# GLA values with tokens on partitions, and their grid rows regrouped into columns through DRAM

## The chip, the core and the metric

The kernel runs on one core of one Trainium2 chip. The metric is the device time of one execution in microseconds (us), lower is better.

## What is computed

The reference is one layer of a diffusion backbone over 512 latent tokens (a grid of 8 rows by 64 columns) with a prefix of 256 context tokens, width 1024, all in float32. A SwiGLU half step comes first, then token mixing (an S5 branch and a gated linear attention branch, GLA, on the same normalised input), then a second SwiGLU half step. The change touches the values `v` of the GLA branch:

```python
u_l, q_l, k_l, v_l, r_l, glr_l, ga_l, gb_l = jnp.split(h_lat @ w_in, points, axis=-1)
u_c, q_c, k_c, v_c, r_c, glr_c, ga_c, gb_c = jnp.split(h_ctx @ w_in, points, axis=-1)
...
q_l, k_l, v_l, r_l, glr_l = [to_col_major(t, rows) for t in (q_l, k_l, v_l, r_l, glr_l)]
...
kv = jnp.einsum('bhnjd,bhnje->bhnde', k * jnp.exp(g_last - gc), v)
...
o_intra = jnp.einsum('bhnij,bhnje->bhnie', scores, v)
```

GLA walks the grid column by column, so the latent tokens of `v` (512 tokens by 512 channels) must stand in the order of columns (token `8*w + r` for column `w` and row `r`), while `h` holds them row by row (`64*r + w`). The products above contract over tokens, so `v` is wanted with tokens on the partitions. Context tokens keep their order.

## The kernel before

Every float32 product is split in three: the operands are cut into a high and a low part in fp32r, and high times low, low times high and high times high are added up in PSUM. `h` is kept as `h_hi` and `h_lo`, 128 partitions of channels by 8 blocks `k` by 768 tokens (512 latent, then 256 context). Weights arrive in units of 128 x 1024 floats: SyncE's queue (SP) loads `w_raw` (four slots), GpSimd (POOL) cuts it into `w_hi` and `w_lo` (L1177 and L1180), TensorE (PE) uses them. A unit's load waits until the unit four before has been cut (`w_split`), its cutting waits until PE is done with the unit four before. PSUM's eight banks are four slots of two banks; a job `j` uses slot `j % 4` (`lat(j)` and `ctx_(j)` are its banks), `job_done` counts finished jobs, and `slot_read` says that a slot was read.

The order of the work on each engine is written out by hand. Around the change PE's program is: the gate logits of two passes (L1811), four jobs `v`, the first half `u0` of the S5 input (`input_part(0)`), the jobs `vt`, and then the list `GLA_ORDER`, which begins with `ket 0` (transposes of the decayed keys), `sc 0` (scores, L1846), `u 1`, `kv 0` (keys times values, L1862), `u 2` and so on.

The four jobs `v` (`tall_job`, all matmuls recorded at L1276) hold the weights still and move the tokens: for each of 4 x 8 blocks and 3 parts one matmul over 512 latent and one over 256 context tokens, 96 pairs in all. The result has channels on the partitions. ScalarE (ACT) copies it to `v_t` and puts the grid in column order by the way (`evac_tokens`, L2394 and L2396). Then 24 PE transposes (L1287, the jobs `vt`) turn it, and ACT copies it to `v_sb` (`take_v`, L2441), from where `kv` and later the readout (L1876) take it.

Other transfers through DRAM that the prediction reads: `g_scr` keeps gates (one transfer writes 128 partitions of 512 floats), and `k_scr` keeps S5 kernels, which SP reads with a hand-made pattern whose leading dimension is `CH = 8`:

```python
lags = bass.AP(k_scr.tensor, (b * P + STRIP * g) * 15 * GC, [[GC, CH], [15 * GC, GC], [1, P]])
sp.dma_start(tile[:, 0, g, :], lags).then_inc(here, 16)
```

Of the kernel before, what the change touches and what calls it, by code (L numbers as in the profile page):

```python
# [29 lines left out]
F32 = mybir.dt.float32  # L30
# [6 lines left out]
P = 128  # L37
# [194 lines left out]
def y_load(h, b):  # L232
# [5 lines left out]
              ("ffn1", FFN1_JOBS), ("norm1", 0), ("q0", 1), ("q1", 1), ("glr", 1), ("k", 2), ("z0", 1), ("z1", 1),  # L238
              ("v", 4), ("u0", 1), ("vt", 6), ("gla", GLA_JOBS), ("chunks", 23), ("gb", 6), ("ga", 8), ("merge", len(MERGE_ORDER)),
              ("ma", KD), ("wo", KD), ("ada7", 1), ("wo_b", 4), ("ffn2", FFN2_JOBS),  # L240
# [117 lines left out]
def last_user(n):  # L358

    for name, count, jobs in (("k", 2, JOB["k"]), ("q0", 1, JOB["q0"]), ("glr", 1, JOB["glr"]), ("q1", 1, JOB["q1"]), ("v", 4, JOB["v"]),  # L360
                              ("ga", 8, JOB["ga"]), ("wo", 4, JOB["wo"])):
        if UNIT[name] <= n < UNIT[name] + count:
            return jobs + n - UNIT[name]
# [30 lines left out]
def build(nc, a, out):  # L394
# [4 lines left out]
    x_scr = nc.dram_tensor("x_scr", [P, KD, NL], F32).ap()  # L399
    u_scr = nc.dram_tensor("u_scr", [CH, GC, G, NCH], F32).ap()  # L400
    g_scr = nc.dram_tensor("g_scr", [P, 2 * KD, NL], F32).ap()

# [107 lines left out]
    g_d = place("g_d", [P, NT], F32, at=stream_at + 9 * KB)  # L510
    v_t = place("v_t", [P, 4, NT], F32, at=ut_at)
    gate_buf = place("gate_buf", [P, 2, NL], F32, at=v_at + 8 * KB)
# [225 lines left out]
    with ExitStack() as es:  # L738
        def sem(name):
            return es.enter_context(nc.semaphore(name))  # L740
# [61 lines left out]
        hc_hi_ok = sem("hc_hi_ok")  # L802
        hc_ok = sem("hc_ok")
        xn_ok = sem("xn_ok")
        h_hi_ok = sem("h_hi_ok")
# [76 lines left out]
        def product_done(eng, q, i):  # L882

            eng.wait_ge(product_ok, NPROD * q + i + 1)

        def block_consumed(eng, b):
# [35 lines left out]
        def _(sp):  # L922
# [100 lines left out]
            def tall(n, count, c0, c=P):  # L1023
                for q in range(count):
                    unit(n + q, w_in[:, :, c0 + q * P:c0 + q * P + c], raw((n + q) % 4, KD, c))

            def load_gate(t):
                g, s = (gate_a, gate_a_in) if t < KD else (gate_b, gate_b_in)
                sp.dma_start(g[:, t % KD, :], g_scr[:, t, :]).then_inc(s[t % KD], 16)
# [24 lines left out]
            tall(UNIT["k"], 2, C_K)  # L1054
            tall(UNIT["v"], 3, C_V)


            sp.wait_ge(xn_ok, 2 * KD)
            sp.dma_start(x_scr, x[:, :, 0:NL]).then_inc(x_spilled, 16)
            tall(UNIT["v"] + 3, 1, C_V + 3 * P)  # L1060
            tall(UNIT["u"], 4, C_U)
            for q, t in enumerate(R_ORDER):
                tall(UNIT["r"] + q, 1, C_R + t * P)
            tall(UNIT["gb"], 2, C_GB)
# [101 lines left out]
        def _(pool):  # L1166
# [16 lines left out]
            def split(n, cols):  # L1183
                pool.wait_ge(w_here[n % 4], 16 * (n // 4 + 1))
                is_done(pool, last_user(n - 4))
                parts(n % 4, cols, n + 1)
# [75 lines left out]
        def _(pe):  # L1262
# [459 lines left out]

            def input_part(p):

                q, j = p // 2, GJ["u", p]
                n, c = UNIT["u"] + q, slice(NL, NT) if p % 2 else slice(0, NL)
                if p % 2 == 0:
                    pe.wait_ge(w_split, n + 5)
                wait_read(pe, j)
                wh, wl = wv(n % 4, KD, P)  # L1730
                split_mm([(wh[:, k, :], wl[:, k, :], [(h_hi[:, k, c], h_lo[:, k, c], lat(j)[:, 0:c.stop - c.start])])
                          for k in range(KD)]).then_inc(job_done, 1)

# [84 lines left out]
            gate_logits(1)  # L1818
            for q in range(4):
                tall_job("v", q, JOB["v"] + q, NT)  # L1820
            input_part(0)
            for q in range(4):
                was_read(pe, JOB["v"] + q)
            for t in range(6):
                j = JOB["vt"] + t
                wait_read(pe, j)
                for q in range(4):
                    last = transpose(lat(j)[:, P * q:P * q + P], v_t[:, q, P * t:P * t + P])
                last.then_inc(job_done, 1)
            def turn_keys(p):  # L1830
# [19 lines left out]
            def key_values(p):  # L1850
                ti, d = p // 2, p % 2
                was_read(pe, GJ["ket", p])
                order = (4, 5, 0, 1, 2, 3) if d == 0 else (5, 4, 3, 2, 1, 0)
# [321 lines left out]
        def _(act):  # L2175
# [261 lines left out]

            def take_v(t):
                j = JOB["vt"] + t
                is_done(act, j)  # L2440
                act.activation(v_sb[:, t, :], lat(j), ACT.Copy).then_inc(slot_read[j % 4], 1)  # L2441

# [39 lines left out]
            softplus(1)  # L2482
            evac_tokens(JOB["v"], v_t[:, 0, :], NT, P)
            decays(0)
            for q in range(1, 4):
                evac_tokens(JOB["v"] + q, v_t[:, q, :], NT, P)
            decays(1)
            take_u(0)
            for t in range(6):
                take_v(t)  # L2490
            take_keys(0)
# [1377 lines left out]
```

## Time and profile before

| | before |
|---|---|
| median of 3 runs | 1352.38 us (1352.18 to 1355.9) |
| the profiled execution | 1354.73 us, of which the profile's span is 1353.0 us |
| mean granted TensorE clock | 0.997 |
| busy share: PE, DVE, ACT, POOL | 99%, 64%, 29%, 48% |
| DMA | 178.18 MB, mean 132 GB/s |

Times in the rows are us from the start of the span. A row of the timeline merges neighbours of one kind: start, duration, engine, line, operation, output and inputs, count, and in brackets the idle time before it. The duration of a matmul reaches over the start of the next one, since they are pipelined; what a stream of them costs is read from start to start.

### The profile page before, as it was taken

How to read it: one execution, taken by the hardware profiler on the slowest of the kernel's cores; microseconds unless marked ns; L12 is line 12 of the kernel's file. 1: busy time of each engine (PE TensorE's matmuls, PEld its weight loads, DVE VectorE, ACT ScalarE, POOL GpSimd, SP SyncE). 2: the span in 40 equal slices, each digit the busy share in tenths (PEclk: the TensorE clock that was granted, in tenths of full speed). 3: DMA queues.
4: the chain of work that ended last, by engine and by line, in shares of the span. 5: the costliest groups of instructions: out<-in, count | busy, mean ns of one | idle time of the engine just before them, and what ended most of it. 6: DMA issues, size and time to landing. Idle time of an engine off the chain costs nothing.

```text
span 1353.0 us, 21483 instructions
## 1 busy us (share of the span) xinstructions
PE 1335.8 (99%) x8556; PEld 1232.3 (91%) x8556; DVE 864.3 (64%) x1383; ACT 395.8 (29%) x750; POOL 652.2 (48%) x408
## 2 busy tenths in 40 slices
PE   7999999999999999999999999999999999999998
PEld 5899999999999999998888888888998999999997
DVE  5697368468556555537656649926778755555666
ACT  4310010210210110124635321222142555544455
POOL 3164444543543543532732356636567455655554
PEclk9999999999999999999999999999999999999999
DMA  9653354353454344223322479484736233344322
GB/s 319 199 148 91 119 147 125 113 159 115 126 140 134 106 128 152 63 55 109 81 61 51 129 211 260 152 268 145 229 87 199 63 94 94 109 116 114 99 75 82
DMA packets 242798, 178.18 MB, mean 132 GB/s; under 512 B 33288, under 2 KB 219916, under 8 KB 242700
## 3 DMA queue, kind: packets, MB, share of 16 engines
q1 hardware_dynamic: 222640, 145.78, 37.7%
q10 hardware_dynamic: 20060, 31.04, 7.0%
q8 instruction: 68, 1.11, 0.4%
q14 instruction: 30, 0.25, 0.1%
HBM read 156.93 MB, written 19.86 MB: 131 GB/s over the span
## 4 chain that ended last, share of the span: by engine, by line
PE 92%; DVE 4%; ACT 1%; issue 1%; ACTq 0%; DMA 0%; POOL 0%; DVEq 0%; POOLq 0%
PE ps L1276 46%; PE ps L2041 13%; PE ps L1636 13%; PE ps L2100 7%; PE ps L1287 1%; PE ps L1914 1%; DVE ada_acc L2924 1%; DVE ps L3028 1%; PE ps L2127 1%; PE ps L1951 1%; PE ps L1739 1%; PE ps L1531 1%; PE ps L1482 1%; PE ps L1776 1%; ACT squares L2197 0%
## 5 line engine op out<-in xcount | busy, mean ns | idle before, releaser
L1177 POOL TENSOR_SCALAR w_hi<-w_raw 128x1024 fp32r<-128x1024 f32 x128 | 154.7, 1209 | 526.8 <-PE ps L1276 279.4
L1180 POOL TENSOR_TENSOR w_lo<-w_raw,w_hi 128x1024 fp32r<-128x1024 f32 x128 | 325.0, 2539 | 10.7
L1276 PE MATMUL ps<-h_hi,w_lo 128*128 128x384 f32 (+2 forms) x984 | 287.3, 351 | 0.0
L1276 PE MATMUL ps<-h_hi,w_hi 128*128 128x384 f32 (+2 forms) x984 | 283.0, 346 | 0.0
L1276 PE MATMUL ps<-h_lo,w_hi 128*128 128x384 f32 (+2 forms) x984 | 283.0, 346 | 0.0
L1276 PEld LDWEIGHTS ps<-h_hi,w_lo 128*128 128x128 f32 x984 | 175.8, 188 | 14.9 <-issue 4.3
L1276 PEld LDWEIGHTS ps<-h_hi,w_hi 128*128 128x128 f32 x984 | 177.6, 188 | 10.8
L1276 PEld LDWEIGHTS ps<-h_lo,w_hi 128*128 128x128 f32 x984 | 177.8, 188 | 10.4
L1254 POOL TENSOR_TENSOR w_lo<-w_raw,w_hi 128x512 fp32r<-128x512 f32 x90 | 115.8, 1301 | 104.4 <-ACT w_hi L2673 102.9
L2924 DVE SCALAR_TENSOR_TENSOR ada_acc<-ada_w,cs,ada_acc 128x1024 f32<-128x1024 f32 x70 | 114.5, 1671 | 6.0 <-DMA ada_w<-in_ada_w_dram 4.0
L2041 PE MATMUL ps<-h_hi,w_hi 128*128 128x256 f32 x360 | 102.0, 283 | 0.0
L2041 PE MATMUL ps<-h_hi,w_lo 128*128 128x256 f32 x360 | 101.9, 283 | 0.0
L2041 PE MATMUL ps<-h_lo,w_hi 128*128 128x256 f32 x360 | 101.8, 283 | 0.0
L1636 PE MATMUL ps<-act_hi,w_lo 128*128 128x384 f32 (+1 forms) x352 | 94.7, 343 | 0.3 <-DVE x L3303 0.3
L1636 PE MATMUL ps<-act_hi,w_hi 128*128 128x384 f32 (+1 forms) x352 | 94.0, 341 | 0.0
L1636 PE MATMUL ps<-act_lo,w_hi 128*128 128x384 f32 (+1 forms) x352 | 94.0, 341 | 0.0
L2315 ACT ACTIVATE silu<-ps 128x768 f32<-128x768 f32 (+1 forms) x26 | 20.3, 780 | 199.3 <-PE ps L1276 193.0
L2334 ACT ACTIVATE act_hi<-ps 128x768 fp32r<-128x768 f32 (+2 forms) x26 | 20.0, 769 | 190.9 <-DVE ps L3259 190.8
L3301 DVE SCALAR_TENSOR_TENSOR x<-ps,mod,x 128x384 f32<-128x384 f32 (+2 forms) x120 | 49.1, 476 | 31.6 <-PE ps L1636 31.5
L2041 PEld LDWEIGHTS ps<-h_hi,w_lo 128*128 128x128 f32 x360 | 68.9, 191 | 0.3
L2041 PEld LDWEIGHTS ps<-h_lo,w_hi 128*128 128x128 f32 x360 | 68.8, 191 | 0.3
L2041 PEld LDWEIGHTS ps<-h_hi,w_hi 128*128 128x128 f32 x360 | 68.8, 191 | 0.0
(452 smaller groups left out, 2648.1 us busy)
## 6 DMA issues: line engine op xcount, KB each, us to landing
w_raw<-in_ffn_w_gate_dram SPq DMA_DIRECT2D x44, 512.0 KB, 5.0
w_raw<-in_ffn_w_up_dram SPq DMA_DIRECT2D x44, 512.0 KB, 4.1
w_raw<-in_ffn_w_down_dram SPq DMA_DIRECT2D x44, 512.0 KB, 3.9
ada_w<-in_ada_w_dram ACTq DMA_DIRECT2D x32, 512.0 KB, 3.9
w_raw<-in_w_in_dram SPq DMA_DIRECT2D x32, 512.0 KB, 4.1
ada_w<-in_ada_w_dram SPq DMA_DIRECT2D x24, 512.0 KB, 4.0
ada_q<-in_ada_w_dram SPq DMA_DIRECT2D x8, 1024.0 KB, 10.7
c_scr<-cp ACTq DMA_DIRECT2D x16, 288.0 KB, 3.7
```

The lines of the kernel that those rows point to most:

```text
L1177: pool.tensor_scalar(w_hi[:, s, 0:cols], w_raw[:, s, 0:cols], 1.0, 1.0, ALU.mult, ALU.mult)\
L1180: pool.tensor_tensor(w_lo[:, s, 0:cols], w_raw[:, s, 0:cols], w_hi[:, s, 0:cols].bitcast(F32), ALU.subtract).then_inc(w_split, 1)
L1254: pool.tensor_tensor(lo, src, hi.bitcast(F32), ALU.subtract).then_inc(block_lo, 1)
L1276: last = pe.matmul(mv[2], st, mv[part], start=(first and q == 0), stop=(n == len(terms) - 1 and q == 2))
L1287: return pe.transpose(o, i, ident[0:i.shape[0], 0:i.shape[0]])
L1636: last = pe.matmul(bank, st[:, k, c], mv[:, k, cols], start=(k == 0 and r == 0), stop=(k == tiles - 1 and r == 2))
L2041: last = pe.matmul(bank_of(q, bank), st[:, k, :], mv[:, k, :], start=(opens and k == 0 and r == 0), stop=(closes and k == HK - 1 and r == ...
L2100: last = pe.matmul(ps[:, banks[e], :], st[:, k, c], mv[:, f + k, 0:NL], start=(k == 0 and r == 0), stop=(k == 1 and r == 2))
L2315: act.activation(dst, src, ACT.Silu).then_inc(slot_read[jg % 4], 1)
L2334: act.activation(dst, src, ACT.Copy).then_inc(act_hi_ok, 1)
L2924: STT(acc, tile, cs[:, k, v:v + 1], acc, ALU.mult, ALU.add).then_inc(acc_ok, 1)
L3301: ins = STT(x[:, k, c], src, mod[:, g, v:v + 1], x[:, k, c], ALU.mult, ALU.add)
```

## The change

The values are made with `h` held still and the weights moving. The four weight units of `v` are cut the other way: two blocks `k` of 512 columns each, in place of eight blocks of 128 columns. For each unit PE runs over six tiles of 128 tokens, with 2 x 3 matmuls of 512 columns each, 144 in all, into six PSUM banks (three slots) that stay open over the four units. The result has tokens on the partitions, so the 24 transposes go. What the copy by ACT did before, the order by columns, is now made by DMA: ACT copies the four latent tiles to `v_row` as they are, SP writes them to `v_scr` in DRAM in four transfers, with rows of 512 floats put at their place in column order, and when all four have landed SP reads `v_scr` back into `v_sb` in four transfers. The two context tiles are copied to `v_sb` directly. `kv 0` waits for the eight transfers.

```diff
-              ("v", 4), ("u0", 1), ("vt", 6), ("gla", GLA_JOBS), ...
+              ("v", 3), ("v_pad", 2), ("u0", 1), ("u0_pad", 1), ("gla", GLA_JOBS), ...
+    v_scr = nc.dram_tensor("v_scr", [NL, VAL], F32).ap()
-    v_t = place("v_t", [P, 4, NT], F32, at=ut_at)
+    v_row = place("v_row", [P, 4, VAL], F32, at=ut_at)
+        def values_read(q):
+            return q + 1 if q < 3 else 6
+        def values_made(m):
+            return 4 + m
+            def value_unit(q):
+                n = UNIT["v"] + q
+                unit(n, w_in[:, 2 * q:2 * q + 2, C_V:C_V + VAL], raw(n % 4, 2, VAL))
+            def turn_values():
+                by_row = v_scr.rearrange("(w r) c -> r w c", r=ROWS)
+                for m in range(2):
+                    was_read(sp, JOB["v"] + m)
+                    for t in (2 * m, 2 * m + 1):
+                        sp.dma_start(by_row[2 * t:2 * t + 2], v_row[:, t, :]).then_inc(v_here, 16)
+                sp.wait_ge(v_here, 16 * 4)
+                for t in range(4):
+                    sp.dma_start(v_sb[:, t, :], v_scr[P * t:P * t + P, :]).then_inc(v_here, 16)
...
             for q, t in enumerate(R_ORDER):
+                if q == 3:
+                    turn_values()
                 tall(UNIT["r"] + q, 1, C_R + t * P)
...
-                is_done(pool, last_user(n - 4))
+                q = n - 4 - UNIT["v"]
+                if 0 <= q < 4:
+                    pool.wait_ge(v_ok, values_read(q))
+                else:
+                    is_done(pool, last_user(n - 4))
...
+            def values():
+                for q in range(4):
+                    n = UNIT["v"] + q
+                    wh, wl = [w[:, n % 4, :].rearrange("p (k c) -> p k c", k=2) for w in (w_hi, w_lo)]
+                    pe.wait_ge(w_split, n + 5)
+                    for t in range(6):
+                        j = JOB["v"] + t // 2
+                        if q == 0 and t % 2 == 0:
+                            wait_read(pe, j)
+                        o = (lat, ctx_)[t % 2](j)
+                        for k in range(2):
+                            for r, (h, w) in enumerate(((h_hi, wl), (h_lo, wh), (h_hi, wh))):
+                                last = pe.matmul(o, h[:, 2 * q + k, P * t:P * t + P], w[:, k, :], start=(q == 0 and k == 0 and r == 0),
+                                                 stop=(q == 3 and k == 1 and r == 2))
+                        if t == 5 or (q == 3 and t % 2 == 1):
+                            last.then_inc(v_ok, 1)
...
-            for q in range(4):
-                tall_job("v", q, JOB["v"] + q, NT)
-            input_part(0)
-            for q in range(4):
-                was_read(pe, JOB["v"] + q)
-            for t in range(6):
-                j = JOB["vt"] + t
-                wait_read(pe, j)
-                for q in range(4):
-                    last = transpose(lat(j)[:, P * q:P * q + P], v_t[:, q, P * t:P * t + P])
-                last.then_inc(job_done, 1)
+            values()
+            input_part(0, JOB["gla"] - JOB["v"])
...
             def key_values(p):
+                if p == 0:
+                    pe.wait_ge(v_here, 16 * 8)
...
+            def take_v(m):
+                j = JOB["v"] + m
+                act.wait_ge(v_ok, values_made(m))
+                dst = v_row[:, 2 * m:2 * m + 2, :] if m < 2 else v_sb[:, 4:6, :]
+                first = act.activation(dst[:, 0, :], lat(j), ACT.Copy)
+                if m == 2:
+                    first.then_inc(slot_read[(j + 1) % 4], 1)
+                act.activation(dst[:, 1, :], ctx_(j), ACT.Copy).then_inc(slot_read[j % 4], 1 if m == 1 else 2)
...
-            evac_tokens(JOB["v"], v_t[:, 0, :], NT, P)
             decays(0)
-            for q in range(1, 4):
-                evac_tokens(JOB["v"] + q, v_t[:, q, :], NT, P)
+            take_v(0)
+            take_v(1)
             decays(1)
+            take_v(2)
             take_u(0)
-            for t in range(6):
-                take_v(t)
```

The instructions themselves show it at three places. On PE, where the values are made, the stream began before with these rows (`h` moves, 512 and 256 wide; brackets hold the semaphores waited for):

```order
L1276 MATMUL ps<-h_hi,w_lo 128x512 [waits slot_read3,w_split]
L1276 MATMUL ps<-h_hi,w_lo 128x256
L1276 MATMUL ps<-h_lo,w_hi 128x512
L1276 MATMUL ps<-h_lo,w_hi 128x256
L1276 MATMUL ps<-h_hi,w_hi 128x512
L1276 MATMUL ps<-h_hi,w_hi 128x256
```

and now begins with these, where the weights move, 512 wide:

```order
L1768 MATMUL ps<-w_lo,h_hi 128x512 [waits slot_read3,w_split]
L1768 MATMUL ps<-w_hi,h_lo 128x512
L1768 MATMUL ps<-w_hi,h_hi 128x512
L1768 MATMUL ps<-w_lo,h_hi 128x512
L1768 MATMUL ps<-w_hi,h_lo 128x512
L1768 MATMUL ps<-w_hi,h_hi 128x512
```

Every pair of 512 and 256 has become one and a half matmuls of 512; the columns moved are as many as before.

On PE between `u0` and `kv 0`, the transposes of `v_t` stood ahead of those of the keys (`ke`):

```order
L1287 MATMUL ps<-ident,v_t 128x128 [waits slot_read0]
L1287 MATMUL ps<-ident,v_t 128x128 x3
L1287 MATMUL ps<-ident,v_t 128x128 [waits slot_read1]
L1287 MATMUL ps<-ident,v_t 128x128 x3
L1287 MATMUL ps<-ident,ke 128x128 [waits slot_read2,e_d]
L1287 MATMUL ps<-ident,ke 128x128 x5
L1846 MATMUL ps<-e1q,kz 128x128 [waits slot_read3,e_d]
L1846 MATMUL ps<-e1q,kz 128x128 x7
```

They are gone, and the first product of keys and values, behind the last matmuls of `u 1`, now waits for the transfers too (`v_here`):

```order
L1308 MATMUL ps<-h_hi,w_lo 128x256
L1308 MATMUL ps<-h_lo,w_hi 128x256
L1308 MATMUL ps<-h_hi,w_hi 128x256
L1905 MATMUL ps<-v_sb,ket 64x128 [waits slot_read1,slot_read2,v_here]
L1905 MATMUL ps<-v_sb,ket 64x128 x11
L1905 MATMUL ps<-v_sb,ket 64x128 [waits slot_read2]
L1905 MATMUL ps<-v_sb,ket 64x128 x11
```

Everything that PE has behind that row stands behind the wait.

On SP's queue, from the loads of the values' weights on, it was (the shape is that of the side written):

```order
L926 DMA w_raw<-in_w_in_dram 128x8x128 [waits w_split] x5
L1059 DMA x_scr<-x 1024x1x512 [waits xn_ok]
L926 DMA w_raw<-in_w_in_dram 128x8x128 [waits w_split] x11
L1070 DMA u_scr<-u_t 16x8x96 [waits slot_read0,slot_read3]
L1070 DMA u_scr<-u_t 16x8x96 x7
```

and is now:

```order
L1085 DMA x_scr<-x 1024x1x512 [waits xn_ok]
L937 DMA w_raw<-in_w_in_dram 128x2x512 [waits w_split]
L937 DMA w_raw<-in_w_in_dram 128x8x128 [waits w_split] x7
L1047 DMA v_scr<-v_row 2x64x512 [waits slot_read3]
L1047 DMA v_scr<-v_row 2x64x512
L1047 DMA v_scr<-v_row 2x64x512 [waits slot_read0]
L1047 DMA v_scr<-v_row 2x64x512
L1050 DMA v_sb<-v_scr 128x512 [waits v_here]
L1050 DMA v_sb<-v_scr 128x512 x3
L937 DMA w_raw<-in_w_in_dram 128x8x128 [waits w_split] x3
L1098 DMA u_scr<-u_t 16x8x96 [waits slot_read0]
```

Eight transfers have moved in ahead of the last three weight loads of this stage, and the four that write have a leading dimension of 2 on the DRAM side.

## Rows read from the trace of the kernel before

**Rows 1.** The page: busy tenths of PE and granted clock in 40 slices.
```profile
PE   7999999999999999999999999999999999999998
PEclk9999999999999999999999999999999999999999
```

**Rows 2.** The chain that ended last, 650 to 700 us: start, us, what.
```profile
653.38 39.62 PE ps L1276 x216
692.99 3.28 PE ps L1287 x30
696.27 1.09 PE ps L1846 x16
```

**Rows 3.** Timeline of PE: first values, `u0`, transposes, keys, `u 1`, `kv 0`.
```profile
653.31 0.62 PE L1276 MATMUL ps<-h_hi,w_lo 128*128 128x512 f32 x2
...
687.32 0.40 PE L1276 MATMUL ps<-h_hi,w_lo 128*128 128x512 f32 x1
...
692.83 2.78 PE L1287 MATMUL ps<-ident,v_t 128*128 128x128 f32 x24
695.45 0.82 PE L1287 MATMUL ps<-ident,ke 128*128 128x128 f32 x6
...
700.34 1.54 PE L1862 MATMUL ps<-v_sb,ket 64*64 64x128 f32 x48
```

**Rows 4.** The chain, 798 to 876 us: a stream of matmuls, all 512 wide.
```profile
798.44 76.24 PE ps L1276 x336
```

**Rows 5.** Weight loads into PE at L1276: ns min/median/max.
```profile
L1276 PEld LDWEIGHTS ps<-h_hi,w_lo x984: 186/188/192, 65.7 to 1035.5; 128*128 128x128 f32 x197
```

**Rows 6.** Timeline of ACT: copies of `v_sb`, and the second pass's decays.
```profile
688.84 0.61 ACT L2432 ACTIVATE g_a<-g_b 128x512 f32<-128x512 f32 x1
...
690.86 0.61 ACT L2436 ACTIVATE g_c<-g_c 128x512 f32<-128x512 f32 x1
...
693.52 3.04 ACT L2441 ACTIVATE v_sb<-ps 128x512 f32<-128x512 f32 x6
```

**Rows 7.** Timeline of POOL: cutting the unit `u2`, before `r2` may load.
```profile
679.17 1.05 POOL L1177 TENSOR_SCALAR w_hi<-w_raw 128x1024 fp32r<-128x1024 f32 x1 [4.38 <-PE ps L1276]
680.31 2.70 POOL L1180 TENSOR_TENSOR w_lo<-w_raw,w_hi 128x1024 fp32r<-128x1024 f32 x1
```

**Rows 8.** Loads of L926 (512 KB each), 640 to 700 us: min/median/max to landing.
```profile
DMA to landing us min/median/max: 3.9/4.0/5.5
```

**Rows 9.** DMA from 862 to 868 us: one gate write of 256 KB, alone.
```profile
GB/s 0 0 0 0 0 0 0 0 0 0 0 0 0 0 0 0 0 0 0 0 55 14 314 382 396 410 219 14 0 0 0 0 0 0 0 0 0 0 0 0
DMA packets 145, 0.27 MB, mean 45 GB/s; under 512 B 16, under 2 KB 16, under 8 KB 144
q10 hardware_dynamic: 144, 0.26, 11.7%
```

**Rows 10.** DMA from 883.3 to 885.0 us: the last four `k_scr` reads (64 KB each).
```profile
DMA  7669554546555656645493444446655435499978
DMA packets 546, 0.28 MB, mean 164 GB/s; under 512 B 32, under 2 KB 545, under 8 KB 545
```

**Rows 11.** Timeline of SP: those four issues, and eight gate reads.
```profile
881.12 2.47 SPq L1043 DMA_DIRECT2D stream<-k_scr  x4
...
902.71 3.66 SPq L1029 DMA_DIRECT2D gate_a<-g_scr  x8
```

**Rows 12.** All DMA issues by line: KB each, median us to landing.
```profile
gate_a<-g_scr SPq DMA_DIRECT2D x8, 256.0 KB, 4.4
```

**Rows 13.** Windows near the start: us, busy (count) PE PEld DVE ACT POOL, PEclk, DMA.
```profile
13.00:16.60 3.60, 0.83 (x5) 0.57 (x5) 2.19 (x6) 3.55 (x9) 1.57 (x2) 1.00 1.10 358
16.60:20.05 3.45, 3.45 (x24) 2.79 (x28) 0.91 (x3) 3.00 (x7) 1.82 (x1) 0.51 1.12 339
20.05:23.50 3.45, 3.42 (x42) 2.22 (x34) 3.45 (x5) 0.77 (x2) 0.71 (x1) 1.00 1.19 298
```

**Rows 14.** Waits of the weight loads, whole span: what PE waited for.
```profile
PEld ps L1951 <- DVE hb L3686: 0.4, 1, 0.4
```

More of the change, by code:

```diff
@@ L238 @@
               ("ffn1", FFN1_JOBS), ("norm1", 0), ("q0", 1), ("q1", 1), ("glr", 1), ("k", 2), ("z0", 1), ("z1", 1),
-              ("v", 4), ("u0", 1), ("vt", 6), ("gla", GLA_JOBS), ("chunks", 23), ("gb", 6), ("ga", 8), ("merge", len(MERGE_ORDER)),
+              ("v", 3), ("v_pad", 2), ("u0", 1), ("u0_pad", 1), ("gla", GLA_JOBS), ("chunks", 23), ("gb", 6), ("ga", 8), ("merge", len(MERGE_ORDER)),
               ("ma", KD), ("wo", KD), ("ada7", 1), ("wo_b", 4), ("ffn2", FFN2_JOBS),
@@ L358, in last_user @@
 def last_user(n):
-    for name, count, jobs in (("k", 2, JOB["k"]), ("q0", 1, JOB["q0"]), ("glr", 1, JOB["glr"]), ("q1", 1, JOB["q1"]), ("v", 4, JOB["v"]),
+    for name, count, jobs in (("k", 2, JOB["k"]), ("q0", 1, JOB["q0"]), ("glr", 1, JOB["glr"]), ("q1", 1, JOB["q1"]),
                               ("ga", 8, JOB["ga"]), ("wo", 4, JOB["wo"])):
@@ L803, in build @@
         hc_ok = sem("hc_ok")
+        v_ok = sem("v_ok")
+        v_here = sem("v_here")
         xn_ok = sem("xn_ok")
@@ L1054, in _ @@
             tall(UNIT["k"], 2, C_K)
-            tall(UNIT["v"], 3, C_V)
+            for q in range(3):
+                value_unit(q)
             sp.wait_ge(xn_ok, 2 * KD)
             sp.dma_start(x_scr, x[:, :, 0:NL]).then_inc(x_spilled, 16)
-            tall(UNIT["v"] + 3, 1, C_V + 3 * P)
+            value_unit(3)
             tall(UNIT["u"], 4, C_U)
             for q, t in enumerate(R_ORDER):
+                if q == 3:
+                    turn_values()
                 tall(UNIT["r"] + q, 1, C_R + t * P)
@@ L1721, in tall_job, with input_part @@
                 split_mm(tall_terms(name, q, j, toks, c)).then_inc(job_done, 1)
-            def input_part(p):
+            def values():
[14 more added lines that the diff above has]
+                            last.then_inc(v_ok, 1)
+            def input_part(p, jobs=1):
                 q, j = p // 2, GJ["u", p]
@@ L1731, in input_part @@
                 split_mm([(wh[:, k, :], wl[:, k, :], [(h_hi[:, k, c], h_lo[:, k, c], lat(j)[:, 0:c.stop - c.start])])
-                          for k in range(KD)]).then_inc(job_done, 1)
+                          for k in range(KD)]).then_inc(job_done, jobs)
             def latents(name, q, j, c, k0, k1):
@@ L2436, in decays @@
                 act.activation(g_c[:, 0:NL], g_c[:, 0:NL], ACT.Exp, scale=1.0 / 16).then_inc(e_a, 1)
[L2438 to L2441, printed above, removed]
+            def take_v(m):
[6 more added lines that the diff above has]
+                act.activation(dst[:, 1, :], ctx_(j), ACT.Copy).then_inc(slot_read[j % 4], 1 if m == 1 else 2)
             def take_keys(p):
```

## The prediction

> **What bounds the kernel now.** I read the page's slices first: PE is at nine tenths or more in 38 of 40, with the clock granted in full [rows 1]. Then the chain of work that ended last, at the place of the change: it runs along PE without a break, 39.62 us of matmuls at L1276, then 3.28 us of transposes, then the scores [rows 2]. So the kernel's time is PE's own time here: whatever PE is spared is saved, and whatever makes PE wait is paid in full, since no other engine stands behind it with work of its own to lose. Third, PE's timeline [rows 3]. It is read from start to start: the values take from 653.31 to 687.32, which is 34.0 us for 96 pairs; `u0` takes 5.51 us to 692.83; the 24 transposes of `v_t` take 2.62 us to 695.45; keys, scores and `u 1` follow, and `kv 0`, the first user of `v_sb`, starts at 700.34.
>
> **What PE is spared.** The 24 transposes go: 2.6 us. The values become 144 matmuls of 512 columns. A stream of such runs 336 times in 76.24 us, 0.227 us each [rows 4], and `u0` ran 24 in 5.51 us, 0.230 each [rows 3]: 32.7 to 33.1 us, I take 32.8. That saves 1.2 us of the 34.0, although the columns are the same. `h` as the operand held still must be loaded for each matmul, but the weights were too, in 188 ns [rows 5], which fits under 227 ns. Together 3.8 us. All that follows would move forward by as much: `kv 0` would be due at 696.5.
>
> The Trainium skill (TensorE: Matmul & The Clock Gate, section Back-to-back issue gap) gives the isolated gap between matmuls as columns over 2.4 GHz plus 2.5 ns. By it the old stream would be 31.2 us and the new 31.1, so that the regrouping alone gave 0.1 us; the rows show 34.0 and 32.7 at least, so I go by the rows.
>
> **Work of other engines.** ACT loses the copies to `v_t` and gets six of about 0.5 us [rows 6], fewer than before; POOL cuts the same units. The values' banks are complete at 680.6, 683.4 and 686.1 (the fourth unit runs from 677.9 to 686.1, two tiles each 2.7 us). ACT needs about 1.1 us for each of the two latent pairs, so slots are released at 681.9 and 684.6. The second pass's decays (2.6 us from 688.84 to the end of the row at 690.86 [rows 6]) come behind them and then the context pair, at about 688.4; the slot that `ket 0` wants at 691.6 is free by then. None of this reaches PE. DVE's instructions are the same.
>
> **The eight transfers.** SP must first issue the load of unit `r2`, which waits until `u2` is cut. That cut took 3.8 us from its start at 679.17 [rows 7]; it now starts at 677.9, so the load is issued at 681.8 and its data is through at about 685.2 (4.0 us to landing [rows 8], less a little for the completion). The writes of tiles 0 and 1 are issued at 682 behind it in the same queue, those of 2 and 3 at 684.7.
>
> How long do the writes take? A gate write of the same size and the same rows of 2 KB, alone in its window, moves 128 packets of data and 16 under 512 B, and uses 11.7% of 16 engines over 6.0 us: 11.2 us of one engine's time, at up to 410 GB/s [rows 9]. The 16 small packets I take for one completion by each engine that took part. Spread over 16 engines that is 0.7 us. But the `k_scr` reads, whose pattern in DRAM leads with a dimension of 8, look otherwise: in 1.7 us the last four leave 32 small packets beside 513 others (4 x 128 rows of 512 B), eight each and not sixteen, and the DMA row stands at about half [rows 10]. They were issued within 2.5 us [rows 11] and drained together, and still only half the engines worked: each takes eight engines, and the four take the same eight. So a transfer here uses as many engines as the leading dimension allows, and a second one gets no others. The four writes of `v_row` lead with 2 (`2x64x512`, two grid rows). I therefore expect them on two engines, all four on the same two: 4 x 11.2 / 2 = 22.3 us.
>
> The Trainium skill (DMA: Bandwidth & Descriptors, section Why a DMA increments its semaphore by 16 and not by 1) says that a transfer issued from SP runs on the largest number of engines up to 16 that divides the leading dimensions of both sides, and on the lowest-numbered ones. The 32 small packets agree with it. By that rule 2 and 128 give two engines, and the writes take the same 22.3 us.
>
> Then the sum: the writes have the two engines from about 685.2 to 707.5, landed 707.8. SP issues the four reads (128 partitions, all engines); eight such reads were issued in 3.66 us [rows 11], landing 4.4 us after issue at the median under each other's load [rows 12]. Between 2.6 us (1 MB at 410 GB/s and nothing else) and 5.8 us (three issues of 0.46 and 4.4) I take 4.2: `v_sb` is there at 712.0, while `kv 0` was due at 696.5. PE stands still for 15.5 us; behind it in its queue is everything else, so the stall is paid in full. Nothing makes it up: SP's later loads `r3` and `gb` are held to 708 as well, but PE wants them only some 50 us further on.
>
> **The clock.** PE does not stand still for so long anywhere in this trace. After sparse work (0.83 us busy of 3.60) and a wait, the granted clock was 0.51 for 3.45 us, the lower of the two levels, 1.2 GHz, and then 1.00 again [rows 13]. I expect one such stretch when PE starts again: 3.45 us at half pace, 1.7 us lost. Bounds: nothing, and two stretches, 3.4 us.
>
> **Sum.** -3.8 + 15.5 + 1.7 = +13.4 us. The profile's own span of 1353.0 would be 1366.4; its execution took 1354.73, 2.35 us above the median of the runs. Against the median of 1352.38 I forecast 1366 us.
>
> **The rivals.**
> *The writes spread.* If they ran on all 16 engines, each takes 0.7 us of transfer, they land before 688 and `v_sb` is there by 693, ahead of 696.5. The same if eight engines serve them (5.6 us, reads landed at about 695.5), or if each write had a pair of its own. Then only the 3.8 us remain: 1348.6. For it speaks that the count of 2 lies outside what the trace shows (the least dimension seen is 8) and that I know the pattern from the program's text; against it the 32 small packets and the half-used engines [rows 10]. It decides at 6.8 us for the four writes: from 685.2 they then land at 692.3, the reads at 696.5, and nothing is exposed; at about 10.6 us the stall would just eat the 3.8.
> *The writes use two engines each, but at another pace.* The 2 KB rows might go at 410 GB/s over 16 engines, the peak of [rows 9]: 20.5 us for the four. Or at the pace of [rows 10] (256 KB on 8 engines in 1.7 us, 19.3 GB/s an engine): 27.2 us. I take [rows 9], the same shape and direction. The ends: 20.5 us of writes, 2.6 of reads and no clock loss give a stall of 12.1 and +8.3; 27.2, 5.8 and 3.4 give a stall of 22.0 and +21.6.
> *The operand exchange is slower than the rows say.* If `h` held still cost more than 227 ns, say 5% of 32.8, then 1.6 us more; with the writes hidden that is 1350.2, no measurable change. Loads of 188 ns speak against it [rows 5].
> *DVE becomes the bound.* PE waits only 0.4 us for the S5 scan (`hb`) [rows 14]. But the scan starts from PE's results too, and moves with them: no price.
>
> **How the numbers follow.** Two engines, all four writes on them: 0.88. Spread or otherwise hidden: 0.09, of which half is measured as over 0.3% faster, since 3.8 us is 0.28%. Something between (partly exposed, near zero): 0.03. A measurement tells 0.3%, 4.1 us, from no change. Faster 0.05, same 0.06, slower 0.89. The likeliest case's own range is 1360 to 1371: its lower end is the cheap bounds, its upper leaves out most of the way to +22, since the packets of [rows 9] have the shape in question. It holds about 9 in 10 of that case, which makes 8 in 10 of all.
>
> **What would show it.** In the profile after: 144 matmuls of 512 at 0.227 us and no `v_t`; `u0` starting near 686.1; four writes landing 13 to 23 us after their issue, with the DMA share near an eighth; a gap of some 15 us on PE before `kv 0` at about 696.5, put down to DMA; a granted clock of 0.5 behind it; all later stages as before. I am wrong if the writes land in 2 to 4 us, each with 16 small packets, or if PE's gap is under 8 us.

## The result, and the profile after

The changed kernel takes 1369.17 us (median of 6 runs, 1367.95 to 1372.63); the kernel before took 1353.99 us in its 6 runs beside it (1352.18 to 1355.9). The ratio is 1.0114, with a 95% interval of 1.0100 to 1.0127: slower by some 15.4 us. The profiled execution, 1372.51 us, is one of the longer of the six; its span is 1370.8 us, against 1353.0 before.

The page of the changed kernel, PE and granted clock in 40 slices, and the chain that ended last by engine:

```profile
PE   6999999999999999999949999999999999999998
PEclk8999999999999999999979999999999999999999
...
PE 91%; DVE 4%; DMA 2%; ACT 1%; issue 1%; ACTq 1%; SPq 1%; POOL 0%; DVEq 0%; POOLq 0%
```

One slice is 34 us. Where all slices but the first and the last were 9 [rows 1], one now is 4, and the clock beside it 7. All the rest is as before, so the question has one place. The chain of the changed kernel there, 650 to 725 us (start, us, what):

```profile
654.62 24.76 PE ps L1768 x108
...
679.53 1.89 POOL w_hi L1205
...
681.49 2.73 POOL w_lo L1208
...
684.23 0.37 SPq L937
...
684.64 0.64 SPq L1047
...
685.33 1.10 SPq L1047
...
686.48 3.64 SPq L1047
...
690.16 18.46 DMA v_scr<-v_row
...
708.63 0.35 SPq L1050
...
709.98 5.26 DMA v_sb<-v_scr
...
715.28 2.84 PE ps L1905 x48
718.12 6.58 PE ps L1308 x24
```

The chain leaves PE at 679.4 and comes back to it at 715.28. It goes over POOL's cut of `u2`, SP's load of `r2` behind it (L937), the four writes (L1047), 18.46 us of waiting for the last of them, and the four reads (L1050). Then `kv 0` (L1905) starts, and takes 2.84 us where it took some 1.5 [rows 3]. What PE waited for (us in total, times, longest):

```profile
PEld ps L1905 <- DMA v_sb<-v_scr: 17.7, 1, 17.7
PE ps L1905 <- DMA v_sb<-v_scr: 17.5, 1, 17.5
```

The windows of the same stretch (busy and count of PE, PEld, DVE, ACT, POOL; granted clock, DMA share, GB/s):

```profile
688.00:693.00 5.00, 5.00 (x24) 4.09 (x24) 0.00 (x0) 1.45 (x3) 3.14 (x2) 1.00 0.13 51
...
698.00:703.00 5.00, 0.00 (x0) 0.00 (x0) 1.88 (x2) 0.19 (x1) 3.99 (x2) 1.00 0.13 51
703.00:708.00 5.00, 0.00 (x0) 0.00 (x0) 0.00 (x0) 0.00 (x0) 0.00 (x0) 0.50 0.13 51
...
715.00:720.00 5.00, 4.72 (x53) 4.00 (x54) 2.65 (x8) 0.00 (x0) 0.00 (x0) 0.50 0.38 104
720.00:725.00 5.00, 5.00 (x26) 4.13 (x25) 2.34 (x5) 0.26 (x1) 0.00 (x0) 1.00 0.00 0
```

Read the last two columns first. From 688 to 708 the DMA engines are 0.13 busy, two of sixteen (0.125), and move 51 GB/s, some 26 GB/s for each of the two. Then the column before them: PE stopped at 697.75, the granted clock is 0.50 (1.2 GHz) from 703 on, and still is for nearly five microseconds after PE has started again. How many engines a write took can be counted too. DMA of 683 to 709 us:

```profile
DMA packets 1560, 1.57 MB, mean 60 GB/s; under 512 B 24, under 2 KB 1048, under 8 KB 1560
```

In that window `r2`'s load and the four writes end. 24 small packets are 16 for the load and 8 for the writes, two each.

### The profile page after: what moved, and what is told of

Same layout as the page of the kernel before. It is cut to its first block, busy times and chain, and to the rows that moved or that the text cites. A ratio compares the mean times of both kernels' runs of the same rounds, so it can differ in the third digit from the quotient of the medians.

```text
span 1370.8 us, 21334 instructions
## 1 busy us (share of the span) xinstructions
PE 1334.5 (97%) x8484; PEld 1231.4 (90%) x8484; DVE 865.0 (63%) x1383; ACT 390.3 (28%) x742; POOL 653.6 (48%) x408
## 4 chain that ended last, share of the span: by engine, by line
PE 91%; DVE 4%; DMA 2%; ACT 1%; issue 1%; ACTq 1%; SPq 1%; POOL 0%; DVEq 0%; POOLq 0%
PE ps L1308 43%; PE ps L2084 13%; PE ps L1668 13%; PE ps L2143 7%; PE ps L1768 2%; PE ps L1563 1%; DMA v_scr<-v_row 1%; PE ps L1319 1%; PE ps L1957 1%; DVE ada_acc L2970 1%; DVE ps L3074 1%; PE ps L2170 1%; PE ps L1994 1%; PE ps L1789 1%; PE ps L1514 1%
## 5 line engine op out<-in xcount | busy, mean ns | idle before, releaser
L1308 PE MATMUL ps<-h_hi,w_lo 128*128 128x384 f32 (+2 forms) x920 | 271.0, 352 | 0.0
L1308 PE MATMUL ps<-h_hi,w_hi 128*128 128x384 f32 (+2 forms) x920 | 266.8, 347 | 0.0
L1308 PE MATMUL ps<-h_lo,w_hi 128*128 128x384 f32 (+2 forms) x920 | 266.7, 347 | 0.0
L1308 PEld LDWEIGHTS ps<-h_hi,w_lo 128*128 128x128 f32 x920 | 166.3, 188 | 13.3 <-issue 3.9
L1308 PEld LDWEIGHTS ps<-h_hi,w_hi 128*128 128x128 f32 x920 | 168.0, 188 | 9.3
L1308 PEld LDWEIGHTS ps<-h_lo,w_hi 128*128 128x128 f32 x920 | 168.1, 188 | 8.9
L2358 ACT ACTIVATE silu<-ps 128x768 f32<-128x768 f32 (+1 forms) x26 | 20.3, 780 | 199.3 <-PE ps L1308 193.0
L2084 PEld LDWEIGHTS ps<-h_hi,w_lo 128*128 128x128 f32 x360 | 68.9, 191 | 0.3
L2084 PEld LDWEIGHTS ps<-h_lo,w_hi 128*128 128x128 f32 x360 | 68.8, 191 | 0.3
L2084 PEld LDWEIGHTS ps<-h_hi,w_hi 128*128 128x128 f32 x360 | 68.8, 191 | 0.0
```

Of the source, the lines that this page charges most:

```text
L1308: last = pe.matmul(mv[2], st, mv[part], start=(first and q == 0), stop=(n == len(terms) - 1 and q == 2))
L2084: last = pe.matmul(bank_of(q, bank), st[:, k, :], mv[:, k, :], start=(opens and k == 0 and r == 0), stop=(closes and k == HK - 1 and r == ...
L2358: act.activation(dst, src, ACT.Silu).then_inc(slot_read[jg % 4], 1)
```

## The experiments

One theory and its rivals ran through them. The theory: the leading dimension of a transfer sets how many DMA engines it runs on, and the data of the most loaded engine go through at 26 GB/s. The rivals: the round trip through DRAM is late by itself; rows that lie 16 KB apart are slow to write; the many issues cost SP the time; another queue would use other engines. Ratios are to the kernel before, with their 95% intervals.

**Writes of single grid rows.** Same bytes to the same places, but each transfer leads with 64.

```diff
-                    for t in (2 * m, 2 * m + 1):
-                        sp.dma_start(by_row[2 * t:2 * t + 2], v_row[:, t, :]).then_inc(v_here, 16)
-                sp.wait_ge(v_here, 16 * 4)
+                    for r in range(4 * m, 4 * m + 4):
+                        sp.dma_start(by_row[r], v_row[64 * (r % 2):64 * (r % 2) + 64, r // 2, :]).then_inc(v_here, 16)
+                sp.wait_ge(v_here, 16 * 8)
...
-                    pe.wait_ge(v_here, 16 * 8)
+                    pe.wait_ge(v_here, 16 * 12)
```

> Each of the four writes of two grid rows (2x64x512) becomes two writes of one grid row (64x512, 128 KB); the reads stay. Theory (a transfer runs on as many engines as its leading dimension allows, 2 before, 16 now): the eight writes take about 0.35 us of 16 engines each, landed some 4 us after the last is issued, so v_sb is complete near PE's due time and the stall of 17.5 us before kv 0 is 0 to 3 us; no stretch at clock 0.5. Time about 3.8 us under before's, 1350, ratio to before 0.997, at most 1.000. Rival 1 (the round trip through DRAM itself is late, or rows of 2 KB that lie 16 KB apart in DRAM are slow): 128 rows of 2 KB are written to the same places, so the writes still take some 20 us and the time stays at ratio 1.011. Rival 2 (more issues cost SP what the engines save): eight issues of 0.6 to 5 us hold SP until past 700, stall 5 to 15 us, ratio 1.002 to 1.010.

Measured: 1351.53 us, ratio 0.9976 (0.9964 to 0.9988). Its chain, 650 to 760 us:

```profile
653.81 32.91 PE ps L1768 x144
686.72 5.44 PE ps L1308 x24
...
693.91 3.05 PE ps L1308 x24
696.96 1.47 PE ps L1905 x48
698.43 5.71 PE ps L1308 x24
```

PE never leaves the chain: `kv 0` follows `u 1` at once, at full clock. SP's timeline, and the DMA packets of 683.8 to 690.8 us:

```profile
683.83 5.09 SPq L1047 DMA_DIRECT2D v_scr<-v_row  x8
690.76 1.77 SPq L1050 DMA_DIRECT2D v_sb<-v_scr  x4
```

```profile
DMA packets 1680, 1.57 MB, mean 225 GB/s; under 512 B 144, under 2 KB 1168, under 8 KB 1680
```

144 small packets are 16 for the load of `r2` and 128 for eight writes, sixteen each. The writes are through 6.9 us after the first was issued, not 24.0. Both rivals fall: the same round trip costs nothing, and eight issues took 5.09 us, half of what four took before.

**No transfers at all.** ScalarE copies straight to `v_sb`. This kernel leaves out the order by columns, so it doesn't compute what the reference does; only its time is read.

```diff
-                dst = v_row[:, 2 * m:2 * m + 2, :] if m < 2 else v_sb[:, 4:6, :]
+                dst = v_sb[:, 2 * m:2 * m + 2, :]
...
-                    turn_values()
+                    pass
...
-                    pe.wait_ge(v_here, 16 * 8)
+                    pass
```

> Leaves out the regrouping of grid rows into columns: ScalarE copies all four value tiles straight to v_sb, the eight transfers and the wait on them are gone, everything else is the change's. It prices the operand exchange and the missing transposes alone. Theory (my terms): 2.6 us of transposes and 1.2 us of values are saved and nothing is lost, 3.8 us under before, ratio 0.9972 (0.9965 to 0.998). Rival (the exchange of the operands costs something that the trace hides, such as h held still loading slower): ratio 0.999 or above. If the whole loss of the change came from elsewhere than the transfers, the ratio would still be 1.011.

Measured: 1349.89 us, ratio 0.9966 (0.9954 to 0.9979). The chain has the same pieces as the run above, 43.15 us from the first value to `kv 0`:

```profile
651.67 32.91 PE ps L1768 x144
...
696.29 5.71 PE ps L1308 x24
```

So the exchange of the operands and the missing transposes are worth 47.03 - 43.15 = 3.9 us [rows 3], and the interval reaches from 2.8 to 6.2. The whole loss of the change lies in the transfers. The intervals of this run and of the one before it overlap, and both take 43.15 us over this stretch: done by grid rows, the transfers cost nothing here that can be measured.

**Near rows, still two by two.** The scratch tensor gets 65 rows for each grid row, so that a grid row's data lie together. This kernel too leaves out the order by columns: `v_sb` then holds rows of the grid.

```diff
-        v_scr = nc.dram_tensor("v_scr", [NL, VAL], F32).ap()
+        v_scr = nc.dram_tensor("v_scr", [ROWS, GRID_W + 1, VAL], F32).ap()
...
-                by_row = v_scr.rearrange("(w r) c -> r w c", r=ROWS)
...
-                        sp.dma_start(by_row[2 * t:2 * t + 2], v_row[:, t, :]).then_inc(v_here, 16)
+                        sp.dma_start(v_scr[2 * t:2 * t + 2, 0:GRID_W, :], v_row[:, t, :]).then_inc(v_here, 16)
...
-                for t in range(4):
-                    sp.dma_start(v_sb[:, t, :], v_scr[P * t:P * t + P, :]).then_inc(v_here, 16)
+                for r in range(8):
+                    sp.dma_start(v_sb[64 * (r % 2):64 * (r % 2) + 64, r // 2, :], v_scr[r, 0:GRID_W, :]).then_inc(v_here, 16)
...
-                    pe.wait_ge(v_here, 16 * 8)
+                    pe.wait_ge(v_here, 16 * 12)
```

> The scratch tensor is laid out as [8 grid rows, 65, 512], so that a grid row's 64 rows of 2 KB lie side by side in DRAM; the four writes still lead with a dimension of 2, and eight reads bring single grid rows back. It leaves out the column order: v_sb holds rows of the grid and not columns. Theory (engine count from the leading dimension): the writes still run on two engines, 20 us, and the time is that of the change, ratio to before 1.009 to 1.013. Rival (the scattered places, 16 KB apart, are what makes the writes slow): with rows side by side the writes take 1 to 3 us and the ratio is 0.997 to 1.000.

Measured: 1371.52 us, ratio 1.0127 (1.0108 to 1.0145). Its chain, and a window:

```profile
690.83 18.49 DMA v_scr<-v_row
```

```profile
700.00:705.00 5.00, 0.00 (x0) 0.00 (x0) 0.36 (x1) 0.00 (x0) 2.56 (x1) 0.57 0.13 51
```

18.49 us, 0.13 and 51 GB/s, as with rows 16 KB apart. Where the rows lie in DRAM made no difference.

**62 and 2, 61 and 3, 57 and 7.** Each grid row is written by two transfers, split as the numbers say; only the pair of numbers differs.

```diff
-                    for t in (2 * m, 2 * m + 1):
-                        sp.dma_start(by_row[2 * t:2 * t + 2], v_row[:, t, :]).then_inc(v_here, 16)
-                sp.wait_ge(v_here, 16 * 4)
+                    for r in range(4 * m, 4 * m + 4):
+                        for a0, a1 in ((0, 62), (62, 64)):
+                            p0 = 64 * (r % 2)
+                            sp.dma_start(by_row[r, a0:a1], v_row[p0 + a0:p0 + a1, r // 2, :]).then_inc(v_here, 16)
+                sp.wait_ge(v_here, 16 * 16)
...
-                    pe.wait_ge(v_here, 16 * 8)
+                    pe.wait_ge(v_here, 16 * 20)
```

> Each grid row is written by two transfers, of 62 and of 2 partitions, 16 writes in all. Two forms of the theory are told apart: by the one a transfer takes the largest number of engines up to 16 that divides the leading dimension (62: two engines, as 2), so the data still go through two engines, the writes take about 20 us and the ratio to before is about 1.011, somewhat more if SP's sixteen issues hold it up. By the other it takes 16 or the leading dimension, whichever is less (62: sixteen), the writes land within 3 to 6 us of the last issue and the ratio is 0.997 to 1.003. For both: small packets of completion counted beside the data, 2 for a transfer by the first, 16 by the second.

> As the run with 62 and 2 partitions, but 61 and 3: 61 is a prime number, so by the divisor rule nearly all data go through one engine. Theory: about 1 MB at 26 GB/s is some 40 us instead of 20, v_sb complete near 730, a stall of 33 to 40 us and 2.4 us of half clock: ratio to before 1.024 to 1.029. Rival (the run with 62 was slow for its sixteen issues or for its small writes of 2 partitions and not for the count of engines): the writes take as long as with 62, ratio 1.011 to 1.015.

> Each grid row is written by two transfers, of 57 and of 7 partitions. 57 is 3 times 19, so by the divisor rule the large one runs on three engines and the small one on seven. The most loaded engine carries 8 x (57/3 + 1) rows of 2 KB, 320 KB, at 26 GB/s 12.6 us, where the change's two carry 512 KB each in 20.2. Theory: the stall is 17.5 - 7.6 = 9.9 us and the stretch at half clock remains, as the run with half the dose had it (8.8 us and a clock of 0.5 behind): -3.8 + 9.9 + 2.4 = 8.5, ratio to before 1.0063 (1.005 to 1.008). Rival (any split into an odd number runs on one engine, or sixteen small issues cost the time): the time of the run with 62 or 61, 1.0137 or 1.0266; or, if 57 rows spread over all engines, 0.9976.

Measured: 62 and 2, 1372.12 us, ratio 1.0137 (1.0116 to 1.0159); 61 and 3, 1390.37 us, 1.0266 (1.0248 to 1.0284); 57 and 7, 1364.02 us, 1.0074 (1.0057 to 1.0091). What PE waited for, in this order:

```profile
PE ps L1907 <- DMA v_sb<-v_scr: 17.9, 1, 17.9
```

```profile
PE ps L1907 <- DMA v_sb<-v_scr: 36.0, 1, 36.0
```

```profile
PE ps L1907 <- DMA v_sb<-v_scr: 9.5, 1, 9.5
```

And one window each of the first two, while the writes ran:

```profile
700.00:705.00 5.00, 0.00 (x0) 0.00 (x0) 0.00 (x0) 0.00 (x0) 0.00 (x0) 0.50 0.13 51
```

```profile
705.00:710.00 5.00, 0.00 (x0) 0.00 (x0) 0.00 (x0) 0.00 (x0) 0.00 (x0) 0.50 0.07 26
```

For 57 and 7, the window in which the last writes ran, and the DMA packets of 683 to 703 us:

```profile
695.00:700.00 5.00, 3.75 (x38) 3.42 (x34) 4.11 (x6) 0.90 (x3) 1.09 (x1) 1.00 0.20 77
```

```profile
DMA packets 1632, 1.57 MB, mean 79 GB/s; under 512 B 96, under 2 KB 1120, under 8 KB 1632
```

62 partitions go through two engines (0.13, 51 GB/s), 61 through one (0.07, 26 GB/s), 57 through three (77 GB/s, three times 26), 64 through sixteen. The small packets say the same. For 57 and 7 they are 96: 16 for the load of `r2` and 80 for eight pairs of writes, three and seven each. From the load to the last write the run with 62 and 2 has 48, which is 16 and eight times 2 + 2, and the run with 61 and 3 has 48 too, 16 and eight times 1 + 3. All three runs have sixteen issues, so it isn't their number that sets the wait. Nor is the count of engines the smaller of 16 and the dimension: it is the dimension's largest divisor up to 16. The Trainium skill (DMA: Bandwidth & Descriptors, section Why a DMA increments its semaphore by 16 and not by 1) states for transfers issued from SP that it is the largest number up to 16 that divides the leading dimensions of both sides; the packets and shares here agree for 64, 62, 61, 57, 7, 3 and 2.

**Half the dose.** Tiles 0 and 1 by pairs of grid rows, tiles 2 and 3 by single ones.

```diff
                     for t in (2 * m, 2 * m + 1):
-                        sp.dma_start(by_row[2 * t:2 * t + 2], v_row[:, t, :]).then_inc(v_here, 16)
+                        if m == 0:
+                            sp.dma_start(by_row[2 * t:2 * t + 2], v_row[:, t, :]).then_inc(v_here, 16)
+                        else:
+                            for r in (2 * t, 2 * t + 1):
+                                sp.dma_start(by_row[r], v_row[64 * (r % 2):64 * (r % 2) + 64, t, :]).then_inc(v_here, 16)
-                sp.wait_ge(v_here, 16 * 4)
+                sp.wait_ge(v_here, 16 * 6)
...
-                    pe.wait_ge(v_here, 16 * 8)
+                    pe.wait_ge(v_here, 16 * 10)
```

> Tiles 0 and 1 are written as in the change (two writes of 2x64x512), tiles 2 and 3 by grid rows (four writes of 64x512): half the dose. Theory (data through two engines at some 26 GB/s each, as the change's trace shows): 512 KB take 10 us from 684, so the writes land at about 695 in the change's time, the reads at 699 to 701.5, kv 0 due at 697.5: a stall of 1.5 to 4 us, no clock loss or a small one, and the 3.8 us saved just pay it: ratio to before 0.998 to 1.001. Rival (any two-engine transfer among them delays all, or the loss has a fixed part that doesn't go with the bytes): a stall of 8 us or more, ratio 1.004 to 1.011.

Measured: 1360.71 us, ratio 1.0047 (1.0030 to 1.0064), and

```profile
PE ps L1909 <- DMA v_sb<-v_scr: 8.8, 1, 8.8
```

This lies outside what I had expected of the theory, and within the rival's range. The fault was in my start: I counted the writes from 684, their issue in the changed kernel. But `r2`'s load is ahead of them on every engine until 688, as the windows of the changed kernel show, and the reads took 6.5 us and not 4. Shifted so that the first value is made when it was in the change, the two engines have 11.3 us of data from 688 (the four other writes put 32 KB on each of them too), the last write is seen at 700, the reads at 706.5, and `kv 0` is due at 697.75: 8.8. That it goes with the bytes is shown by the runs together. The wait is worked out here as 17.5 us less what the most loaded engine is spared of the change's 512 KB, at 26 GB/s:

| run | KB on the most loaded engine | at 26 GB/s, us | wait by that, us | measured, us |
|---|---|---|---|---|
| single rows, 64 | 64 | 2.5 | 0 | 0 |
| half | 288 | 11.3 | 8.6 | 8.8 |
| 57 and 7 | 320 | 12.6 | 9.9 | 9.5 |
| the change | 512 | 20.2 | 17.5 | 17.5 |
| 62 and 2 | 512 | 20.2 | 17.5 | 17.9 |
| 61 and 3 | 992 | 39.1 | 36.4 | 36.0 |

The run with two queues, below, carries 512 KB as well and waited 16.9 us. The two runs of about half the dose differ in their issues (6 and 16), and fall on the same line. The change's own row fits by construction; the others are off by 0.4 us at most, so no fixed part larger than that goes with writes on few engines. The 9.9 of the run with 57 was worked out before that run was made.

**Two queues.** ScalarE issues the writes of tiles 2 and 3.

```diff
-                for m in range(2):
-                    was_read(sp, JOB["v"] + m)
-                    for t in (2 * m, 2 * m + 1):
-                        sp.dma_start(by_row[2 * t:2 * t + 2], v_row[:, t, :]).then_inc(v_here, 16)
+                was_read(sp, JOB["v"])
+                for t in (0, 1):
+                    sp.dma_start(by_row[2 * t:2 * t + 2], v_row[:, t, :]).then_inc(v_here, 16)
...
+                if m == 1:
+                    by_row = v_scr.rearrange("(w r) c -> r w c", r=ROWS)
+                    was_read(act, j)
+                    for t in (2, 3):
+                        act.dma_start(by_row[2 * t:2 * t + 2], v_row[:, t, :]).then_inc(v_here, 16)
```

> The writes of tiles 2 and 3 are issued by ScalarE in its own queue, behind its copies; those of tiles 0 and 1 stay with SyncE. Theory (the leading dimension sets the number of engines and it is the same two for every queue): the four writes together still take 20 us on two engines, ratio to before 1.009 to 1.015, above the change's if ScalarE is held up in issuing. Rival (another queue's transfers go to other engines): the two halves run side by side, 10 us, the DMA share is 0.25 and the stall 2 to 5 us: ratio 0.998 to 1.002.

Measured: 1371.80 us, ratio 1.0132 (1.0112 to 1.0153). The wait, and a window in which both queues have writes open:

```profile
PE ps L1904 <- DMA v_sb<-v_scr: 16.9, 1, 16.9
```

```profile
690.00:695.00 5.00, 5.00 (x27) 4.04 (x27) 0.00 (x0) 3.07 (x7) 2.45 (x2) 1.00 0.13 51
```

Still 0.13 and 51 GB/s: the second queue's writes go to the same two engines.

**A clock kept up.** PE gets work in place of the pause: 76 matmuls into a bank that `kv 0` then overwrites.

```diff
                 if p == 0:
+                    wait_read(pe, GJ["kv", p])
+                    for _ in range(76):
+                        pe.matmul(lat(GJ["kv", p]), h_hi[:, 0, 0:P], h_hi[:, 0, 0:NL], start=True, stop=True)
                     pe.wait_ge(v_here, 16 * 8)
```

> The change, plus 76 matmuls of 512 columns on h_hi into kv 0's own bank (overwritten by it), between PE's last matmul and the wait for v_sb: 76 x 0.227 = 17.3 us of work in place of the idle 17.5. It adds work that the reference doesn't ask for. Theory (4.8 us at clock 0.5 behind the pause cost 2.4 us): the clock stays at 1.00, kv 0 takes 1.47 us and not 2.84, u2's 24 matmuls 5.7 and not 6.6, and the time is 2.4 us below the change's, ratio to before 1.0095. Rival (the granted clock falls for another reason, such as the DMA traffic): 0.5 is still granted from 703 on, and as the filling then runs at half pace too, the time is some 10 us or more above the change's, ratio 1.018.

Measured: 1366.36 us, ratio 1.0089 (1.0073 to 1.0105). A window of the former pause, with the writes running, and the chain behind it:

```profile
700.00:705.00 5.00, 5.00 (x24) 4.14 (x23) 0.00 (x0) 0.00 (x0) 0.00 (x0) 1.00 0.13 51
```

```profile
712.19 1.54 PE ps L1908 x48
713.73 5.68 PE ps L1308 x24
```

The granted clock stays at 1.00 although the same writes run, so it is PE's standing still that lowered it. `kv 0` and the 24 matmuls behind it take 7.2 us in place of 9.4 in the changed kernel: the clock cost it 2.2 us. The two ratios' intervals touch, so the trace and not the timing gives this number.

**The reads alone.** SP waits for the four reads before it loads `r3` and `gb`.

```diff
                     sp.dma_start(v_sb[:, t, :], v_scr[P * t:P * t + P, :]).then_inc(v_here, 16)
+                sp.wait_ge(v_here, 16 * 8)
```

> The change, and SyncE waits for its four reads of v_scr before it issues the loads of r3 and gb behind them (those are held 5 us more; PE wants them some 50 us later). In the change the reads took 6.6 us from the first issue, with 1 MB of loads issued directly behind them. Theory (the loads share the engines with the reads and delay them; alone they take 4 to 4.5 us): v_sb is complete 2 us earlier, the stall is 15.5 and not 17.5, ratio to before 1.0100, 2 us below the change's. Rival (the reads' time is their own, three issues and the landing): still 6.6 us, stall 17.5, ratio 1.0114 or, if the later loads become late for PE, more.

Measured: 1370.22 us, ratio 1.0128 (1.0113 to 1.0143), not told from the change's 1.0114. Its chain:

```profile
705.58 0.35 SPq L1050
...
706.92 4.20 DMA v_sb<-v_scr
...
711.16 2.84 PE ps L1906 x48
714.00 6.90 PE ps L1309 x24
```

The reads take 5.5 us from the first issue (705.58 to 711.12) instead of 6.6, and PE waits 16.7 us instead of 17.5. That alone doesn't show that the loads behind them delay the reads. In the other runs that wait for the same four reads, all with `r3` and `gb` issued right behind, these took, from the first issue to the landing that lets `kv 0` start, 5.35 us (61 and 3), 5.6 (57 and 7), 5.7 (two queues), 6.2 (62 and 2, and the filled pause), 6.5 (half the dose) and 6.6 (the change). So 5.5 can be had with the loads behind, and this one execution doesn't decide between the theory and its rival. The forecast of 4 to 4.5 us for reads alone failed. Nor does the microsecond show in the time; part goes to the clock, since the 24 matmuls of `u2` take 6.90 us here and 6.58 in the changed kernel.

## Why the prediction was right, step by step

The forecast was 1366 us, slower, by writes that run on two engines. Times below are set to the execution of before: in the profiled one of the change the first value is made at 654.55 instead of 653.31 [rows 3], 1.2 us later, for reasons ahead of the change.

- **What PE is spared:** 3.8 forecast, 3.9 measured, from the first value to `kv 0`'s due time. 144 matmuls take 32.91 us, 0.229 each; forecast 32.8. The gap rule of the Trainium skill (TensorE: Matmul & The Clock Gate, section Back-to-back issue gap) made 31.1 of it and a saving of 0.1 in the regrouping; neither is what the chain shows.
- **`kv 0` due at 696.5:** 697.75 less 1.2. Right.
- **Two engines, the same two for all four:** right, and shown by the packets (two for each write), the share (0.13), and the runs with 64, 62, 61 and 57 partitions and with the second queue.
- **The writes' time:** 22.3 us forecast from the one gate write [rows 9] (11.2 times four over two is 22.4), 20.3 measured (688.0 to 708.3), near the rival's 20.5 from the peak of the same rows. They started 1.6 us later than forecast. POOL's cut of `u2` took 4.7 us instead of 3.8 [rows 7], 1.89 for `w_hi` where I had read 1.05, and the load of `r2` kept the engines busy for 3.8 us from its issue and not 3.4; the cut also began 0.4 later. So the landing came out within 0.4 us of the forecast (708.6 against 709.0) by two errors that cancel, which is luck: the writes were forecast 2.0 us too long and 1.6 too early.
- **The reads:** the term that was mis-sized. 4.2 us forecast, 6.6 measured, over my upper bound of 5.8. With nothing behind them they took 5.5, and with the loads behind them between 5.35 and 6.6 in different runs, so what the loads add is not shown. The median landing of gate reads [rows 12] counts from the issue of each, and my bound of 5.8, three issues and one such landing, is near what most runs took; the 4.2 was a choice between two bounds and came out too low.
- **The stall:** 15.5 forecast, 17.5 measured: the reads' 2.4 less the 0.4.
- **The clock:** 1.7 forecast, 2.2 measured. One stretch at 0.50, as said, but 4.8 us long behind the restart and not 3.45 (3.5 to 5.4 in the other runs that paused).
- **Sum:** +13.4 forecast; -3.9 + 17.5 + 2.2 = +15.8 by the trace, +15.4 by the ratio. The rest of the distance from 1366 to 1369.17 is the kernel before, whose median was 1353.99 in these runs and not 1352.38.
- **The rivals:** writes on 16 engines would be 1348.6; made so, the kernel takes 3.2 us less than before by its ratio, forecast 3.8. `h` held still cost nothing. DVE never became the bound.

What stays open: why the four reads take 5.35 us at the least, and up to 6.6, with loads behind them or not. It wasn't tried with single reads.

## What to carry to other kernels

Look at the leading dimension of both sides of every transfer that something waits for. If the largest number up to 16 that divides both is small, the data go through as few engines as that, and further transfers of the kind add to the same engines. Split it so that each part leads with a multiple of 16: the eight writes of one grid row, with twice as many issues, made a kernel faster than both (0.9976 of before). And count such a transfer from when the loads ahead of it are through, not from its issue.

## What the runs showed of the hardware that I had not expected

- SP is held in issuing to few engines. The four writes of 256 KB took 0.64, 1.10, 3.64 and 4.97 us to issue; eight of 128 KB to sixteen engines 0.60 each; in the run with 61 and 3 partitions, from the third pair on, the issue of each large write took 0.5 us and that of the small one behind it 4.35. One pair follows the other by 5.0 us, near the 4.9 that its 124 KB on the one engine take at 26 GB/s. ACT's two, the only ones on its queue, took 1.49 together.
- 26 GB/s for an engine with rows of 2 KB, within 1 GB/s, whether one, two or three engines ran and wherever the rows lay.
- The stretch at half clock after the restart cost between 1.6 us (`u2`'s 24 matmuls in 5.98, the run with half the dose) and 2.6 us (6.90, the run with the reads alone), and `kv 0` took 2.84 each time. A pause of 8.8 us brought it as surely as one of 36.
- Executions of nearly the same program differed by up to 5.0 us in when the first value was made (650.90 to 655.86), with the stage behind it equal to 0.1 us. Differences of this size are read within a stage, not between spans.
